# Mixer tiles 2 and 3 of a hybrid streaming encoder: input also loaded channel-major as bf16, row factors spread by ones matmuls of diagonals

## The reference

```python
def rmsnorm(x, g):
    x32 = x.astype(jnp.float32)
    y = x32 * lax.rsqrt(jnp.mean(jnp.square(x32), axis=-1, keepdims=True) + EPS)
    return (y * g.astype(jnp.float32)).astype(x.dtype)

    # sub-layer 1: parallel head groups (pooling | short gated conv), sandwich-normed
    xn = rmsnorm(x, g_mix_pre)                 # x: (B, T, 1024)
    proj = xn @ w_in                           # (B, T, 2048)
    u, bg, cg, h = split(proj)                 # 512 columns each
    y_pool = pool_mix(u_ext, ...)              # trailing means minus u, then a 128x128 map per group
    y_conv = bg * conv3(cg * h)                # depthwise, causal, width 3
    merged = concat(group_rmsnorm(y_pool), group_rmsnorm(y_conv))
    x = x + rmsnorm(merged @ w_out, g_mix_post)
    # sub-layer 2: cross-attention into 256 memory tokens; sub-layer 3: squared-ReLU MLP, width 4096
```

## Time and profile before

| | us |
|---|---|
| median of 3 runs (849.96 to 850.24) | 850.08 |
| the profiled execution, slowest core | 849.38 |
| its span, first to last instruction, core 1 | 847.8 |
| spans of the 8 cores | 842.9 to 847.8 |
| PE busy in the span | 817.6 |
| DVE busy | 388.9 |
| ACT busy | 390.7 |
| POOL busy | 82.4 |

### The profile page before, as it was taken

The page is one execution under the profiler, slowest core; times in us unless marked ns, Lnnn a source line. Parts: engine busy times, 40 slices in busy tenths (PEclk is TensorE's granted clock), DMA queues, the critical chain, the costliest instruction groups (busy, mean ns, idle before and its releaser), DMA issues.

```text
span 847.8 us, 13852 instructions; the slowest of 8 cores (842.9 to 847.8 us)
## 1 busy us (share of the span) xinstructions
PE 817.6 (96%) x4724; PEld 393.3 (46%) x4724; DVE 388.9 (46%) x539; ACT 390.7 (46%) x806; POOL 82.4 (10%) x163
## 2 busy tenths in 40 slices
PE   2899999999999999999999999999999999999997
PEld 0444454444644455455554454444444444444443
DVE  3896886568965667565222222241222321222112
ACT  3587786758866657565332223332233411233101
POOL 5712103002100002000010000000000000000000
PEclk9999999999999999999999999999999999999999
DMA  9999339640495607993899716881249820185011
GB/s 187 199 236 212 104 108 232 119 72 1 76 159 92 199 27 206 161 162 82 143 147 162 186 63 140 155 148 53 92 107 152 154 68 26 49 152 97 1 50 50
DMA packets 29792, 102.38 MB, mean 121 GB/s; under 512 B 2386, under 2 KB 13266, under 8 KB 24348
## 3 DMA queue, kind: packets, MB, share of 16 engines
q0 software_dynamic: 19408, 67.32, 45.9%
q1 hardware_dynamic: 9740, 32.75, 11.2%
q10 hardware_dynamic: 576, 1.44, 0.5%
HBM read 144.38 MB, written 18.07 MB: 192 GB/s over the span
## 4 chain that ended last, share of the span: by engine, by line
PE 89%; DMA 7%; DVE 2%; issue 1%; ACT 1%; POOL 0%; ACTq 0%; DVEq 0%; POOLq 0%
PE ps L668 86%; DMA wdn<-w_down 4%; PE ps L673 3%; DMA XT<-xt 2%; DMA up<-w_up 1%; DVE sAB L1042 0%; DVE X L723 0%; DVE pld L723 0%; POOL wdn L742 0%; DVE Am L733 0%; DVE O L704 0%; ACT rf L697 0%; DVE mg L723 0%; PE ps L873 0%; ACT O L697 0%
## 5 line engine op out<-in xcount | busy, mean ns | idle before, releaser
L668 PE MATMUL ps<-wdn,hid 128*128 128x512 bf16 x1024 | 222.3, 379 | 1.6 <-DMA wdn<-w_down 1.6
L668 PE MATMUL ps<-xT,up 128*128 128x512 bf16 x1024 | 222.6, 379 | 0.0
L668 PEld LDWEIGHTS ps<-wdn,hid 128*128 128x128 bf16 x1024 | 99.8, 98 | 121.2 <-issue 2.0
L668 PEld LDWEIGHTS ps<-xT,up 128*128 128x128 bf16 x1024 | 99.6, 98 | 119.2 <-issue 0.2
L704 DVE TENSOR_TENSOR O<-ps,gp 128x1024 f32<-128x1024 f32 (+1 forms) x49 | 58.4, 1201 | 193.4 <-PE ps L668 132.9
L697 ACT ACTIVATE rt<-ps 128x512 bf16<-128x512 f32 x128 | 76.4, 597 | 142.5 <-PE ps L668 137.8
L668 PE MATMUL ps<-xT,win 128*128 128x512 bf16 x512 | 124.9, 390 | 16.4 <-DMA win<-w_in 14.8
L704 DVE TENSOR_TENSOR hid<-rt 128x512 bf16<-128x512 bf16 x128 | 54.5, 425 | 158.2 <-ACT rt L697 156.4
L697 ACT ACTIVATE sqj<-ps 128x1024 bf16<-128x1024 f32 (+1 forms) x33 | 32.8, 995 | 175.8 <-PE ps L668 173.4
L668 PEld LDWEIGHTS ps<-xT,win 128*128 128x128 bf16 x512 | 50.1, 99 | 76.0 <-issue 23.1
L742 POOL DMA_DIRECT2D up<-w_up x32 | 17.3, 542 | 507.6 <-PE ps L668 494.4
(11 more groups left out here) (182 smaller groups left out, 655.1 us busy)
## 6 DMA issues: line engine op xcount, KB each, us to landing
up<-w_up POOLq DMA_DIRECT2D x32, 1024.0 KB, 9.6
x<-X SPq DMA_DIRECT2D x16, 512.0 KB, 4.1
X<-x SPq DMA_DIRECT2D x16, 512.0 KB, 4.7
wdn<-w_down POOLq DMA_DIRECT2D x8, 1024.0 KB, 30.2
yp<-X SPq DMA_DIRECT2D x15, 512.0 KB, 2.6
X<-xp POOLq DMA_DIRECT2D x8, 512.0 KB, 44.1
X<-xp SPq DMA_DIRECT2D x8, 512.0 KB, 4.0
win<-w_in POOLq DMA_DIRECT2D x4, 768.0 KB, 27.6
```

What stands on the lines that cost most here:

```text
L668: P.add([("pe", lambda e, L: e.matmul(L(out), lhsT=lhsT, rhs=rhs, start=start, stop=stop, skip_group_check=True), max(0.03, n * 0.000421 + ...
```

## The change

The host passes one more array, `xt23`: tiles 2 and 3 with channels on partitions and all eight chunks beside each other. `load_turned` loads it with a cast into `xT[0]` and `xT[1]` as soon as the last readers of tile 0 and tile 1 have gone. `pre_turned` takes the place of `pre_tile(2, 0, ...)` and `pre_tile(3, 0, ...)`: it computes the four sub-tiles' row factors from the row-major X as before, splits them into three bf16 parts that add up to the factor (`rb`), multiplies the identity by each (`dg`, 128 x 1536 bf16, on GpSimd), and with three ones matmuls gets a PSUM tile in which every partition holds the 512 factors. Eight multiplies then scale `xT` in place by column gain and factor. The row-major X of tiles 2 and 3 is loaded as before; `pre_tile` stays for tile 1 and for the later sub-layers.

```diff
+    xt23 = din("xt23", [2, 128, 8 * TN])
+    dg = at("dg", hids.off, 3 * TN, BF16)
+    rb = rot("rb", 1, 3 * NSUB, BF16)[0]
+    def load_turned(t):
+        load(xT[t % 2][:, :], xt23[t - 2], 2097152, q="pool", desc=16384)
+
+    def pre_turned(t):
+
+        n = NSUB
+        ss, ln, rs, rem = (stat(128, n) for _ in range(4))
+        for i in range(n):
+            act(xsr[xs_n[0] % 2][:, :], Xof[(t, i)], AF.Square, accum=ss[:, i:i + 1])
+            xs_n[0] += 1
+        act(ln, ss, AF.Ln, scale=1.0 / D, bias=epsb[:, 0:1])
+        act(rs, ln, AF.Exp, scale=-0.5)
+        left = rs
+        for q in range(3):
+            b = rb[:, q * n:(q + 1) * n]
+            copy(b, left)
+            if q < 2:
+                tt(rem, left, b, ALU.subtract)
+                left = rem
+        tt(r3(dg[:, :], 3 * n), idb[:, :].unsqueeze(1).to_broadcast([128, 3 * n, 128]),
+           rb[:, :].unsqueeze(2).to_broadcast([128, 3 * n, 128]), ALU.mult, eng="pool")
+        ps = PS(1)
+        for q in range(3):
+            mm(ps.v(0, 128, 0, TN), ones[:, :], dg[:, q * TN:(q + 1) * TN], q == 0, q == 2)
+        for kc in range(8):
+            x = xT[t % 2][:, kc * TN:(kc + 1) * TN]
+            stt(x, x, gcs[:, kc:kc + 1], ps.v(0, 128, 0, TN), ALU.mult, ALU.mult)
@@ the order of the first stage
     for cc in range(4):
         ext_conv(cc)
         step(conv_group(0, cc))
+    load_turned(2)
     pre_tile(1, 0, xT[1], junk)
...
     step(None)
+    load_turned(3)
     ext_conv_rest()
     kv_mem()
     mix_out(0)
     out_smp(lambda kc: mgs[:, kc * NS:(kc + 1) * NS], 8, wo)
-    pre_tile(2, 0, xT[0])
+    pre_turned(2)
     mix_out(1)
...
             if cc == 1 and t + 1 < NT:
-                pre_tile(t + 1, 0, xT[(t + 1) % 2])
+                pre_turned(t + 1)
```

More of the change, by code:

```diff
@@ L543, in dout @@
         return nc.dram_tensor(name, list(shape), F32, kind="ExternalOutput")
-    xp = din("xp", [TP, D]); xt0 = din("xt0", [4, 128, 1024]); xe = din("xe", [NX, D])
+    xp = din("xp", [TP, D]); xt0 = din("xt0", [4, 128, 1024]); xt23 = din("xt23", [2, 128, 8 * TN]); xe = din("xe", [NX, D])
     spool = din("spool", [32, 512]); sconv = din("sconv", [4, 512])
@@ L1582 @@
         d["xt0"] = halves(x_prompt[b, t0:t0 + TN])
+        d["xt23"] = f(x_prompt[b, t0 + 2 * TN:t0 + 4 * TN].reshape(2, TN, 8, 128).transpose(0, 3, 2, 1).reshape(2, 128, 8 * TN))
         halo = f(x_prompt[b, t0 - XH:t0]) if half == 1 else np.zeros((XH, D), np.float32)
```

## The result

The changed kernel takes 861.0 us in the median of 5 runs (859.2 to 861.37) against 850.24 us for the kernel before in 5 runs. The ratio is 1.0124 with a 95% interval of 1.011 to 1.0138. It is 10.8 us slower, where I had forecast 848.2 and had set 852.0 as the upper end. The profiled execution took 860.81 us with a span of 859.1 on its slowest core, 11.3 us more than the span before.

A forecast was written before the change was run, and what follows sets the result against it. PE's own instruction stream was taken as the bound: 2.31 us less PE work plus a 0.4 us wait gave -1.9 us, so 850.1 became 848.2 us, range 846.6 to 852.0.

The forecast's parts named there:

- ScalarE: ACT in tiles 2 and 3: squares stay, row scalings and three of four Ln/Exp pairs go; not the bound, counted nothing.
- POOL: GpSimd product of identity and spread factors: 2.8 us, upper bound 3.7; `V`/`vh` copies and load issues queue behind; counted nothing.
- the loads: Two new 2 MB turned loads, 9.6 us each, landing at 85 to 95 and near 115 us; cost zero.
- rival (1): Entry of tile 2: DVE posts delay the in-place multiplies, PE waits 5.8 us, 853.6 us in all; chance 0.17.
- a fresh order that goes badly elsewhere: New plan loses time somewhere other than the entry of tile 2, at about 852 us; chance 0.03.
- The PE work: Tiles 2 and 3: transposes removed 3.60 us, `ones` matmuls added 1.29 us, net 2.31 us less on PE.
- rival (3): POOL product and DVE posts block each other at each tile; 1.4 us lost at tile 2, 849.2 us; chance 0.08.
- The chain at the entry of tile 2: From last square to first `xT` chunk 8.0 us, the other seven 4.6 us; chunk 7 there at 134.4 to 136.7.
- the five tiny DVE operations: Tiny copies and subtractions on DVE splitting the factors, within the wait for tile 2's first chunk: 0.8 us.
- 0.4 us for the entry: PE's expected wait for tile 2's last chunk, taken near the covered end of 0 to 1.0 us.
- an X reload of over 6 us: Sign that the forecast is wrong: reloads of row-major X taking over 6 us, against 4.0 us for one.
- After 190 us: DVE nearly full there; its work waits for PE's matmuls, so it starts earlier with PE; no loss counted.

The follow-up runs named there:

- e1: Changed kernel with both copies into `sT` recorded before both DMAs out of it, at both state outputs: 848.08 us, ratio 0.9989 to the kernel before.
- e5: Changed kernel in its own recording order, `sT` moved to 2 KB of its own: 847.77 us, ratio 0.9984 to the kernel before.
- e2: Kernel before, with only the two waits of the second `sT` copies for the pool_s and pool_p DMAs added: 861.99 us, ratio 1.0149.
- e6: Kernel before with the two turned loads added, `pre_tile` writing over what they bring: 848.42 us, ratio 1.0000.
- e8: Changed kernel, both dependencies kept, planner's fixed time for pool_s and pool_p DMAs raised from 2.6 to 9.4 and 7.7 us: 848.49 us, ratio 0.9999.
- e4: Changed kernel with copies into `sT` before the DMAs and only tile 3 turned by the host: 849.53 us, ratio 1.0002 to the kernel before.
- e9: Changed kernel, `sT` copies before DMAs, planner's fixed time for two `w_v` loads 9.0 instead of 2.6 us: 848.35 us, ratio 0.9987 to kernel before.

## Why the prediction was wrong

**The step that failed.** Under ScalarE I wrote what goes and "so I count nothing"; under POOL and the loads I named what queues behind them; nowhere did I ask what already lay on the bytes that `dg` takes. The diff says `hids.off`, the kernel's own listing says `sT = at("sT", hids.off, ...)`, and each of the four copies of state into `sT` is made on ACT and followed by a DMA. Those were two added waits on an in-order queue whose work PE needs all along, and the sum had no term for them. In place of that nothing the slowest core showed 11.8 us of holes and 3.9 us of lowered clock, and taking the waits away (e1, e5) gave back 1.35 and 1.40% of the time, some 12 us. My rival (1) had a hole at the entry of tile 2 with a price of 5.8 us and a chance of 0.17, but by another mechanism; e1 and e2 show that its mechanism isn't what cost the time. The 0.03 for "a fresh order that goes badly elsewhere", at 852, is the only case near it, and far too small.

**The PE work.** Right: 58 fewer matmul records (4666 against 4724), which is 64 transposes less and 6 matmuls more. The saving of 2.31 us in work is the same in every variant that turns both tiles; e1 and e5 keep 1.0 and 1.3 us of it in the median (849.12 to 848.08, 849.07 to 847.77). By the spans of all eight cores, averaged over the runs, it is 1.4 and 1.5 us (845.0 to 843.6 in both). Without the false dependency the measured gain is 0.1 to 0.2%, below the 0.2% that I had called the least that can be told from no change.

**GpSimd.** The product took 2.74 and 3.09 us where I took 2.8, from this view of `dg` (ns min/median/max):

```profile
L708 POOL TENSOR_TENSOR dg<-idb,rb x2: 2743/2918/3092, 128.4 to 178.7; 128x1536 bf16<-128x1536 bf16 x2
```

The slope of the earlier trace rows was a good guide, and the Trainium skill's 2.6 cycles an element (GPSIMD Engine Reference, 3.1 Elementwise), an estimated 3.3 us, was above both. The blocking of rival (3) was not seen at this cost.

**The chain at the entry of tile 2.** Its size was wrong and its consequence right. From the last square to the first chunk I had 8.0 us; it took 133.25 - 121.65 = 11.6. The term most mis-sized is the five tiny DVE operations. I gave them 0.8 us and 0.6 for one operation in front of them. In the trace the posts of the output tile stand between them, as rival (1) had it (DVE in order of time):

```profile
124.59 0.16 DVE L735 CAST rb<-st 128x4 bf16<-128x4 f32 x1
124.66 1.22 DVE L706 TENSOR_TENSOR O<-ps,gp 128x1024 f32<-128x1024 f32 x1
125.80 0.15 DVE L706 TENSOR_TENSOR st<-st,rb 128x4 f32<-128x4 f32 x1
126.05 0.17 DVE L735 CAST rb<-st 128x4 bf16<-128x4 f32 x1
126.64 1.28 DVE L725 SCALAR_TENSOR_TENSOR X<-O,st,X 128x1024 f32<-128x1024 f32 x1 [0.42 <-ACT st L699]
127.84 0.15 DVE L706 TENSOR_TENSOR st<-st,rb 128x4 f32<-128x4 f32 x1
128.10 0.17 DVE L735 CAST rb<-st 128x4 bf16<-128x4 f32 x1
...
132.51 6.71 DVE L725 SCALAR_TENSOR_TENSOR xT<-xT,cst,ps 128x512 bf16<-128x512 bf16 x8 [2.81 <-PE ps L675]
```

From 124.59 to 128.27 they took 3.7 us. The eight multiplies came every (6.71 - 0.75) / 7 = 0.85 us instead of 0.66. Chunk 7 was there at 139.2, not at 134.4 to 136.7. And yet PE waited there only 0.78 us for ACT's `xs` and 0.26 for `xT`, because the plan did what I had thought possible: all `wkv` filler first, then single matmuls of several groups as the chunks arrive. In e1 its slowest core waited another 1.65 us for a `w_v` load at 148 us, since the filler had been spent early; four of the eight cores had such a wait of over 0.4 us. I took 0.4 us for the entry, and 2.7 were missed there on that core, 1.0 where the load was in time.

**The loads.** Cost zero was right (e6), and for the reason given: the first landed at 94.1, where I had 85 to 95, and the second at 116.7, where I had 115, though it took 12.6 us and not 9.6. One sign of being wrong that I had named, an X reload of over 6 us, was worth nothing: the three reloads issued after 125 us took 7.0 to 14.3 us, and in the kernel before three took 8.0 to 13.0. I had read only the median, 4.0.

**After 190 us.** I had said that DVE's full stretch would move along. It did: PE misses 0.17 us in 190 to 235 us in both the changed kernel and e1, against 1.76 before.

## What to carry to other kernels

When a change puts a new tile on old bytes, list everything else that lives on them, and every wait that the tracker will draw from it, on rows that never meet too; then ask which in-order queue each waiting instruction heads. A wait costs what stands behind it, not what it is for: the same dependency cost some 12 us where the planner believed 2.8 us and about nothing where it was told 9.6 (e8). Look up the landing time of a DMA in the trace, at its own place and with what is in flight beside it, instead of scaling it by its bytes or taking a median. Don't count on the whole of a saving of a microsecond or two on the bound engine when the order is laid out anew: of 2.3 us some 1.4 were kept on the mean of the cores and 1.0 to 1.3 in the metric, one small wait (e4) ate more than the 1.15 us of tile 3, and taking one away (e9) opened two others. And where the metric is the slowest of eight cores, look at all eight before a wait on that core is called the price of an edit.

## What the runs showed of the hardware

A store of 64 KB from 32 partitions took 9.58 us from issue to landing, and one of 32 KB from 16 partitions 7.84 us. Their shape alone does not explain it. In the same stretch of the changed kernel, with a DMA share of 1.02 in 131 to 150 us and two 1 MB `w_v` loads in flight (127.4 to 146.4 and 131.3 to 154.4), the 512 KB x1 store of 128.0 took 13.2 us. And two pairs of stores of one form, 256 KB each, differ by a factor of four in the median (queue, count, KB, us to landing):

```profile
mk<-O SPq DMA_DIRECT2D x2, 256.0 KB, 9.3
mv<-O SPq DMA_DIRECT2D x2, 256.0 KB, 2.1
```

The `mk` stores were issued at 126.5 and 130.5 and took 6.3 and 12.3 us; the `mv` stores were issued at 160.3 and 167.9, where the DMA share is 0.12 (158 to 170 us), and took 2.05 each. The store of 32 KB ran beside a `w_co` load issued half a microsecond ahead of it (DMA share 0.76 in 230 to 240 us). So the landing time went with what else was in flight. Whether few partitions add something of their own is open: no trace times a small store in a quiet stretch. The Trainium skill (DMA: Bandwidth & Descriptors, Latency and other measured facts) puts the fixed cost of a DMA at about 2 us, with HBM's own latency reaching 2 us under high load; the 2.05 us of the quiet stores, bytes included, is near the first, and beside heavy traffic the measured 7.8 to 13.2 us decide. A plan made with 2.6 us for all of it went wrong by a factor of three.

A hole of 7.75 us in PE's work was followed by 3 us at a granted clock of 0.50 and 4 us at 0.78 on average; the hole of 4.05 us by 10 us at 0.85 on average. On that core the low clock added about a third to what the holes cost, 3.9 us to 11.8. On the eight cores of the changed kernel it followed 15 of the 16 holes, those of 2.2 us as well as that of 7.75, and cost 1.3 to 2.5 us each time, with steps of up to 0.43 us from matmul to matmul instead of 0.216. Behind one hole, of 3.1 us on core 6, the clock stayed at 1.00 (149.5 to 153 us). What decides it isn't shown.
